# Both halves of an output projection as seven products instead of eight, in a fused attention and mixture-of-experts kernel

## The reference: what is computed

```
y_na  = neighbourhood_attention(q, k, v, rpb)          # (512 tokens, 512)
y_gla = gla_mixer(...)                                 # (512 tokens, 512)
x = x + concatenate([y_na, y_gla], axis=-1) @ w_out    # w_out: (1024, 1024)
h = rmsnorm(x, norm_ffn_g)
x = x + hierarchical_moe(h, ...)   # top group of 4, top 2 of its 8 experts; 32 experts, SwiGLU, width 512
return rmsnorm(x, final_norm_g)
```

## Time and profile before

| | us |
|---|---|
| median of 3 runs | 741.88 (740.94 to 743.22) |
| the profiled execution | 741.59 |
| its span, first to last instruction | 739.7 |
| PE busy / DVE busy / ACT busy / POOL busy in the span | 725.4 / 251.6 / 146.7 / 77.3 |
| moved by DMA in the span | 240.79 MB |

### The profile page before, as it was taken

The page is one execution under the profiler, slowest core; times in us unless marked ns, Lnnn a source line. Parts: engine busy times, 40 slices in busy tenths (PEclk is TensorE's granted clock), DMA queues, the critical chain, the costliest instruction groups (busy, mean ns, idle before and its releaser), DMA issues.

```text
span 739.7 us, 11649 instructions
## 1 busy us (share of the span) xinstructions
PE 725.4 (98%) x5077; PEld 403.3 (55%) x5077; DVE 251.6 (34%) x516; ACT 146.7 (20%) x315; POOL 77.3 (10%) x79
## 2 busy tenths in 40 slices
PE   9999999999999999999999999999999999999995
PEld 5488888888555564455454454444544544444431
DVE  2884463754873475112012012111111111111205
ACT  2652230134553541000000000000000000000014
POOL 0000049100000310000101001001000010010003
PEclk9999999999999999999999999999999999999999
DMA  9832322214902989999999999999999999999985
GB/s 322 265 113 101 141 103 86 86 67 178 390 2 85 424 293 388 414 429 426 414 419 427 436 431 433 433 428 430 439 414 424 434 424 426 426 427 426 422 362 232
DMA packets 31733, 240.79 MB, mean 326 GB/s; under 512 B 5590, under 2 KB 6998, under 8 KB 21184
## 3 DMA queue, kind: packets, MB, share of 16 engines
q1 hardware_dynamic: 29056, 235.94, 77.7%
q0 software_dynamic: 2480, 4.06, 1.5%
q10 hardware_dynamic: 144, 0.00, 0.0%
HBM read 231.74 MB, written 12.32 MB: 330 GB/s over the span
## 4 chain that ended last, share of the span: by engine, by line
PE 90%; DMA 7%; DVE 1%; ACT 1%; issue 0%; DVEq 0%
PE bank L1164 27%; PE bank L694 17%; PE bank L1184 14%; PE bank L1105 9%; DMA arena<-in_w_all 7%; PE bank L959 4%; PE bank L738 4%; PE bank L1008 4%; PE bank L1118 2%; PE bank L1173 1%; PE bank L997 1%; PE bank L911 1%; PE bank L978 1%; PE bank L1038 1%; PE bank L1219 1%; PE bank L888 1%
## 5 line engine op out<-in xcount | busy, mean ns | idle before, releaser
L1164 PE MATMUL bank<-arena 128*64 128x512 f32 x1024 | 226.7, 593 | 2.4 <-DMA arena<-in_w_all 2.3
L1164 PEld LDWEIGHTS bank<-arena 128*64 128x64 f32 x1024 | 73.4, 137 | 147.2 <-issue 147.0
L694 PE MATMUL bank<-arena 128*128 128x256 f32 x560 | 123.2, 380 | 0.0
L1184 PE MATMUL bank<-arena 128*64 128x512 f32 x512 | 116.9, 598 | 0.2
L694 PEld LDWEIGHTS bank<-arena 128*128 128x128 f32 x560 | 105.7, 190 | 15.5 <-issue 1.5
L1990 DVE SCALAR_TENSOR_TENSOR arena<-bank,arena 128x256 f32<-128x256 f32 x32 | 15.5, 484 | 215.4 <-ACT arena L1488 215.4
L1105 PEld LDWEIGHTS bank<-arena 128*128 128x128 bf16 x1344 | 75.3, 98 | 22.2 <-issue 21.9
L1534 DVE TENSOR_TENSOR arena<-arena 128x512 f32<-128x512 f32 (+8 forms) x105 | 81.2, 809 | 12.6 <-ACT arena L1305 6.1
L1488 ACT ACTIVATE arena<-bank,arena 128x256 f32<-128x256 f32 x32 | 15.2, 474 | 338.1 <-PE bank L1164 332.3
L1105 PE MATMUL bank<-arena 128*128 128x128 bf16 (+1 forms) x1344 | 81.6, 217 | 0.0
L2164 POOL DMA_INDIRECT y_tok<-arena x31 | 30.3, 978 | 402.4 <-DVE arena L1997 374.3
(11 more groups left out here) (179 smaller groups left out, 477.9 us busy)
## 6 DMA issues: line engine op xcount, KB each, us to landing
arena<-in_w_all SPq DMA_DIRECT2D x47, 2048.0 KB, 30.0
arena<-in_w_all SPq DMA_DIRECT2D x7, 6144.0 KB, 26.8
arena<-in_w_all SPq DMA_DIRECT2D x8, 4096.0 KB, 28.2
arena<-in_w_all SPq DMA_DIRECT2D x19, 1024.0 KB, 10.3
arena<-in_w_in SPq DMA_DIRECT2D x5, 2048.0 KB, 8.8
arena<-in_w_all SPq DMA_DIRECT2D x9, 512.0 KB, 7.8
arena<-in_x SPq DMA_DIRECT2D x8, 512.0 KB, 6.4
arena<-in_w_out SPq DMA_DIRECT2D x4, 1024.0 KB, 15.6
```

What stands on the lines that cost most here:

```text
L694: mm = pe.matmul(pbank[product_bank(g, p)][:, tile * 256:(tile + 1) * 256], lhs, rhs, start=(p in (1, 2, 5) and tile == 0 and k == 0), sto ...
L1164: mm = pe.matmul(both, xT[:, k, rows], gate_and_up(e, k)[:, :, cols], start=(k == 0), stop=(k == KC - 1))
L1184: mm = pe.matmul(pbank[down_bank(e)][64 * half:64 * half + 64, :], hidT[:, kc % 2, kc // 2], down_unit(e)[:, kc, half * 512:(half + 1) * 512],
```

## The change

Both halves become seven products of half-size blocks each, as in the input projection.

**GLA half.** For each half h of the 1024 columns, seven products (`SHARE_ORDER`), each of 256 tokens by 256 columns: 2 token tiles x 2 row chunks, 4 matmuls of 256 columns, in bank 4 or 5. 14 shares in 14 of the turns 3 to 18 (`SHARE_TURNS`; none in 8 and 13). DVE makes six sums of weight blocks ahead of the loop, four sums of token blocks in turn 2, one weight difference after each half's product 2, and 14 adds to `x1` (`add_share`), one for each product. To free banks 4 and 5 the scores of a pair of units now share banks 2 and 3, side by side; so the scores of both units wait until both units before have been read.

**Neighbourhood half.** For each pair m of token tiles, seven products (`NEAR_ORDER`), each of 128 tokens by 512 columns: 2 matmuls of 512 columns, 14 products. DVE makes three weight sums (`near_weight_sums`), four token sums per pair (`near_token_sums`, 256 elements in a row each), `last_near_sum`, and 14 adds (`add_near`). A half tile of `x1` is complete with the add named in `LAST_ADD`; in odd tiles the second half is complete first (`half_of`). The order of ScalarE's work stays, but for the last tile, where `hi(3,1)` comes ahead of the eviction. On DVE the order is written anew. On TensorE the new order is in the diff. `router` of the last tile starts with the half that DVE evicts.

**Loads.** Expert 1 waits for `pv_done` alone. Half of expert 2 (`load_half(2,0)`) lies over sums that the new form needs, and waits for product (1,6); other slices are cut and ordered anew.

```
-GLA_BANK = [0] * 6 + [2, 3]
+SHARE_ORDER = [(h, p) for h in range(2) for p in (1, 2, 6, 5, 7, 3, 4)]
+SHARE_TURNS = [3, 4, 5, 6, 7, 9, 10, 11, 12, 14, 15, 16, 17, 18]
+NEAR_ADDS = [(0, 1), (0, 2), (0, 5), (0, 6), (0, 3), (1, 2), (0, 7), (1, 1), (0, 4),
+             (1, 5), (1, 6), (1, 3), (1, 7), (1, 4)]
+LAST_ADD = {(0, 0): (0, 2), (0, 1): (0, 3), (1, 0): (0, 7), (1, 1): (0, 4),
+            (2, 0): (1, 1), (2, 1): (1, 3), (3, 0): (1, 7), (3, 1): (1, 4)}
+def near_bank(m, p):
+    return 2 if p == 2 else 1 if p in (5, 3) else 3 * m
+def half_of(t, n):
+    return n ^ t % 2
...
             sp.wait_ge(pv_done, 4 * PAIRS)
-            sp.wait_ge(og_done, 2 * TT)
             load_half(1, 0)
             load_half(1, 1)
             load_d(1)
-            load_half(2, 0)
-
             over_gla = slice(half_row // 2, half_row)
+            sp.wait_ge(og_done, len(SHARE_ORDER))
             sp.dma_start(flat_half(3, 1)[:, over_gla], half_d(3, 1)[:, over_gla]).then_inc(w2nd_in[3], 16)
+            sp.wait_ge(wo_done, near_product(0, 7))
             sp.dma_start(down_unit(2)[:, 2], down_d(2)[:, 2 * D:3 * D]).then_inc(wd_in[2], 16)
...
             load_over_residual(0)
+            sp.wait_ge(wo_done, max(near_product(0, 4), near_product(1, 1)))
             load_over_yT(0, 2)
+            load_over_w_on(0, 1)
             load_over_residual(1)
+            sp.wait_ge(wo_done, max(near_product(1, 5), near_product(1, 6)))
+            load_half(2, 0)
+            sp.wait_ge(wo_done, near_product(1, 3))
+            load_over_w_on(3, 4)
+            load_over_residual(2)
+            sp.wait_ge(wo_done, len(NEAR_ORDER))
+            load_over_w_on(1, 3)
             load_over_yT(2, 3)
-            load_over_w_on(0)
-            load_over_residual(2)
-            load_over_w_on(1)
             load_over_yT(3, 4)
             load_over_residual(3)
...
             def na_scores(i):
                 pair, b = divmod(i, BLOCKS)
-                if i >= 2:
-                    pe.wait_ge(s_added, 2 * (i - 1))
+                if i >= 2 and i % 2 == 0:
+                    pe.wait_ge(s_added, 2 * i)
...
             def gla_share(n):
+                h, p = SHARE_ORDER[n]
+                if n >= 2:
+                    pe.wait_ge(og_added, n - 1)
+                if p in (3, 4, 5, 6, 7):
+                    pe.wait_ge(sums_done, max(sums("Y", {5: 1, 6: 2, 7: 3}.get(p, 4)), sums(f"share{h}", 4 if p == 4 else 2)))
+                a, w = share_tokens(p), share_weights(h, p)
+                for tile in range(2):
+                    for k in range(2):
+                        mm = pe.matmul(pbank[share_bank(h, p)][:, tile * 256:(tile + 1) * 256], a[:, k, tile * P:(tile + 1) * P],
+                                       w[:, k], start=(p in (1, 2, 5) and tile == 0 and k == 0), stop=(tile == 1 and k == 1),
+                                       skip_group_check=p in (6, 7, 4, 3))
+                mm.then_inc(og_done, 1)
...
+            def out_proj(m, p, ks=range(2)):
+                before = {6: 1, 7: 6, 4: 7, 3: 5}.get(p)
+                if before and ks[0] == 0:
+                    pe.wait_ge(og_added, near_added(m, before))
+                if m == 1 and p in (2, 5) and ks[0] == 0:
+                    pe.wait_ge(og_added, near_added(0, 2 if p == 2 else 3))
+                if p in (3, 4, 5, 6, 7) and ks[0] == 0:
+                    pe.wait_ge(sums_done, max(sums(("y", m), {5: 1, 6: 2, 7: 3}.get(p, 4)), sums("N", 4 if p == 4 else 2)))
...
+            pe.wait_ge(wout_in, 32)
+            pe.wait_ge(yn_evicted, PAIRS // 2)
+            out_proj(0, 1)
             pe.wait_ge(yn_evicted, PAIRS)
+            pe.wait_ge(s_added, 2 * NU)
+            out_proj(0, 2)
+            out_proj(0, 5)
+            out_proj(0, 6)
+            out_proj(0, 3)
+            out_proj(1, 2)
+            out_proj(0, 7)
             x1_T(0)
+            out_proj(1, 1)
+            out_proj(0, 4)
             pe.wait_ge(router_ready, 3)
             router(0)
+            out_proj(1, 5)
             x1_T(1)
+            out_proj(1, 6)
             router(1)
+            out_proj(1, 3)
+            out_proj(1, 7)
             x1_T(2)
+            out_proj(1, 4, range(0, 1))
             router(2)
...
             ranks(0, 2)
+            out_proj(1, 4, range(1, 2))
             last_x1_T(0)
             last_x1_T(1)
...
             def hi(t, n):
+                half = half_of(t, n)
+                act.wait_ge(og_added, x1_half(t, n))
...
             (DVE)
+            near_token_sums(0)
+            add_near(0, 1)
+            add_near(0, 2)
+            add_near(0, 5)
             rest(0, 0)
+            add_near(0, 6)
+            add_near(0, 3)
+            near_token_sums(1)
             rest(0, 1)
+            add_near(1, 2)
+            last_near_sum()
+            add_near(0, 7)
             mean_square(0)
+            x1_T_evict(0)
             rest(1, 0)
+            add_near(1, 1)
             inverse_root(0)
+            add_near(0, 4)
             rest(1, 1)
+            add_near(1, 5)
+            x1_T_evict(1)
             mean_square(1)
+            add_near(1, 6)
             rest(2, 0)
             inverse_root(1)
+            add_near(1, 3)
+            route_groups(0, 2)
             rest(2, 1)
+            add_near(1, 7)
+            x1_T_evict(2)
             mean_square(2)
             route_experts(0, 2)
             rest(3, 0)
             inverse_root(2)
             route_groups(2, 3)
             route_experts(2, 3)
+            add_near(1, 4)
             first_slots(0, 2)
             x1_T_evict(3)
             rest(3, 1)
```

More of the change, by code:

```diff
@@ L140, in second_half_landed @@
 def second_half_landed(e):
-    return landed(e, lambda n: 32 if n == 2 or n in IN_HALVES else 16, 64)
+    return landed(e, lambda n: 48 if n == 2 else 32 if n in IN_HALVES else 16, 64)
 def down_landed(e):
@@ L910, in na_scores @@
                     k0 = KEY_START[b] * ROWS
-                    mm = pe.matmul(pbank[2 + 2 * (i % 2) + par][:, 0:NKEY], na_q[rows, pair, b * P:(b + 1) * P],
+                    mm = pe.matmul(pbank[2 + par][:, i % 2 * NKEY:(i % 2 + 1) * NKEY], na_q[rows, pair, b * P:(b + 1) * P],
                                    na_k[rows, pair, k0:k0 + NKEY], start=True, stop=True)
@@ new lines, in y_sums @@
+            def y_sums():
+                low, high = slice(0, 2), slice(2, 4)
+                dve.wait_ge(yg_evicted, GLA_HEADS)
+                tt(y_sum[1], yT_gla[:, low, late], yT_gla[:, high, late], ALU.add).then_inc(sums_done, 1)
+                tt(y_sum[3], yT_gla[:, low, early], yT_gla[:, low, late], ALU.subtract).then_inc(sums_done, 1)
+                dve.wait_ge(sums_done, sums("Y", 1))
+                tt(y_sum[2], y_sum[1], yT_gla[:, low, early], ALU.subtract).then_inc(sums_done, 1)
+                dve.wait_ge(sums_done, sums("Y", 2))
+                tt(y_sum[4], yT_gla[:, high, early], y_sum[2], ALU.subtract).then_inc(sums_done, 1)
@@ new lines, in add_share @@
+            def add_share(n):
+                h, p = SHARE_ORDER[n]
+                if n == 0:
+                    for t in range(TT):
+                        dve.wait_ge(x_in_sb[t], 32)
+                dve.wait_ge(og_done, n + 1)
+                if n:
+                    dve.wait_ge(og_added, n)
+                tt(share_target(h, p), share_target(h, p), pbank[share_bank(h, p)][:].rearrange("p (t c) -> p t c", t=2),
+                   ALU.add).then_inc(og_added, 1)
+                if p == 2:
+                    dve.wait_ge(sums_done, sums(f"share{h}", 2))
+                    tt(share_quarter(h, 1, 0), share_quarter(h, 1, 0), share_sum[h][2], ALU.subtract).then_inc(sums_done, 1)
@@ L1744, in _ @@
                     scale_probs(1)
+                    y_sums()
                     join(NEAR_V, 5)
@@ L1909, in _ @@
             route_experts(2, 3)
-            residual(3, 1)
+            add_near(1, 4)
             first_slots(0, 2)
@@ L2154, in _ @@
             for t in range(TT):
-                for half in range(2):
-                    pool.wait_ge(mid_done, 2 * t + half + 1)
+                for n in range(2):
+                    half = half_of(t, n)
+                    pool.wait_ge(mid_done, 2 * t + n + 1)
                     nc.gpsimd.tensor_tensor(h2_part[t][2][:, halves[half]], rest2[t % 2][:, halves[half]],
```

208 lines of the change are left out of this document (122 added, 86 removed).

## The result

The kernel after took 749.85 us (median of 6, 748.77 to 751.67), the kernel before beside it 742.55 (6 runs, 740.94 to 744.12): ratio 1.0101, 95% interval 1.0081 to 1.0122. I had forecast 743.0, from 738.5 to 746. The profiled execution took 750.87 (span 749.1). One execution of the kernel before, beside a later experiment, took 4285.84 us; it stands in no ratio.

The account below looks back on a forecast made before the run. The weight queue's deciding issue after the router stage was taken as the bound, TensorE next. Issue +1.05 and expert 0 +1.5 (-3.4 + 0.35 + 4.0 + 0.55) gave +1.2 us: 743.0, range 738.5 to 746.

Parts of the forecast that it names:

- the paragraph on the clock: TensorE ahead of two routers: gaps of 2.75 us leave the clock at 2.4 GHz, so nothing was added.
- rival C: Router stage: the clock falls to half behind two gaps, about +10 us, 753; chance 3%.
- GLA half, work and banks: Score loop: 14 shares of 1.85 us instead of 16 of 1.83, -3.4 us; shared score banks +0.35 us.
- The charge of 0.35 us: Score loop, turn 14: scores come 0.3 us too soon for DVE; +0.35 us charged, bounds 0 and 3 us.
- the waits, places, releasers and sizes: Neighbourhood half: TensorE waits at four places, 2.15, 2.75, 1.35 and 1.95 us, together 8.2 us.
- the stage: First neighbourhood product to expert 0: 231.9 to 279.9 us; to the last transposes 40.5 us, +4.0, then router(3) +0.55.
- the sum: End of the run: deciding issue +1.05, expert 0 on TensorE +1.5; +1.2 us taken.
- the deciding issue: Weight queue after the router stage: the issue from which it never runs dry, moving from 275.58 to 276.6 us, +1.05.
- Rival A: Both halves: the saved work arrives at the end, -6.8 us, 735.1, if all four waits are hidden; chance 15%.
- Rivals B and D: B: DVE sets the score loop's pace, 745.0, 16%. D: weight slices land after 278 us, 2 us late, 745, 5%.

Follow-up runs that it names:

- e2: Kernel after, with ScalarE's three evictions of the transposes moved forward in its queue: 741.96 us, ratio 0.9997 to the kernel before.
- e3: Kernel before, with router(0) also waiting for rest(2,0), a gap of 2.2 us on TensorE: 745.63 us, ratio 1.0061.
- e6: Kernel before, with router(0) also waiting for hi(2,0), a shorter gap of 1.48 us on TensorE: 744.57 us, ratio 1.0041.
- e1: Kernel after, with useless 320-column matmuls in TensorE's four gaps and all waits kept: 744.08 us, ratio 1.0034 to the kernel before.
- e4: Kernel before, with the GLA half of the change alone, the neighbourhood half as before: 738.41 us, ratio 0.9953.
- e5: Kernel after, with ScalarE's three evictions moved ahead and four useless matmuls ahead of the last transposes: 739.42 us, ratio 0.9978 to the kernel before.
- e8: Kernel after, with evictions moved ahead, four useless matmuls, and DVE's route_groups(0,2) ahead of product (1,3)'s add: 738.37 us, ratio 0.9958 to the kernel before.
- e7: Kernel before, with router(0) also waiting for rest(2,0) and three useless matmuls ahead of that wait: 743.35 us, ratio 1.0028.

## Why the prediction was wrong

**The step that failed** is the paragraph on the clock: "Through 4.8 us of standing still it was at 2.4 GHz, so gaps of 2.75 us leave it there, and I add nothing", and with it the 3% of rival C. The row was read rightly: at the end of the run the clock fell 4.8 us after PE's last matmul. The inference was wrong. It took the time from PE's stop to the fall for the length of standing still that a fall needs. In the kernel after, the fall came 2.8, 4.8 and 3.2 us after PE's last record ahead of a gap had ended, in e2 3.0, in e3 and e6 2.7, and all six times PE had taken up work again by then, 0.2 to 2.3 us before: the fall comes behind the gap and does not ask whether it is over. A row in which nothing follows cannot show that. Nor is 4.8 us a fixed length. The same instructions end every run; in e1 the clock fell 3.0 us after the last of them, in the kernel after 5.3, in e6 2.6 (PE's last record ends at 734.62, the fall is at 737.2):
```profile
734.00:737.00 3.00, 0.63 (x2) 0.00 (x0) 1.44 (x3) 2.95 (x6) 2.78 (x2) 1.00 0.54 210
737.00:738.00 1.00, 0.00 (x0) 0.00 (x0) 0.56 (x2) 0.99 (x2) 0.00 (x0) 0.60 0.97 389
```
Rival C had the mechanism, not the price: it put 10 us on two gaps. The clock fell three times, and e1, where it stays, takes 7.3 us off the stage and 5.0 off the end, by the two ratios, whose intervals are some 1.5 and 1.1 us to either side. Its rule, which the prediction named from the Trainium skill ("TensorE: Matmul & The Clock Gate", "Why this matters for your kernels"), that idle gaps between bursts of matmuls bring the clock back to half, is borne out by these runs. The row there speaks of longer gaps than any of these; where it and the runs differ the runs decide, and in e6 1.48 us was enough.

**Right:** GLA half, work and banks. A share takes 1.83 us (the last one runs from 230.17 to 232.00; forecast 1.85), and S is 232.0. The charge of 0.35 us was for scores that wait for DVE at turn 14. They do not wait: the loop loses 0.18 us, and that one turn earlier, where transposes wait for ScalarE's copy:
```profile
215.42 0.63 PE L1065 MATMUL bank<-arena 128*128 128x128 f32 x4 [0.18 <-ACT arena L1512]
```
e4 shows that this part reaches the end whole, within its interval.

**Right:** the waits, places, releasers and sizes. Ahead of router(0) 2.01 (2.15), of router(1) 2.52 (2.75), around x1_T(2) 0.17 + 0.97 = 1.14 (1.35). The last, 1.02 instead of 1.95, is short since PE, at half rate, came late to it; at full clock, in e1, three fillers and 0.46 us stand there, 2.24 us from start to start. In e1 the four come to 8.7 us with the fillers in them, forecast 8.2.

**Off by 0.7 us:** the stage. 48.71 in e1 against 48.0 (279.9 - 231.9); 0.5 of it is in the four gaps. And e1's ratio, 1.0034, is 2.5 us, where the sum gave 1.2; its interval (1.4 to 3.6) leaves out 1.2 by little.

**What the end follows:** the prediction let the deciding issue set it, PE's start of expert 0 second. Over the eleven profiled executions the time less E0 is 462.8 to 464.7 us, the time less the deciding issue 465.6 to 469.3. The odd one is e2: its issue came at 273.48, 2.1 us earlier than before's, expert 0 at 278.59, 0.2 later, and its time equals before's. There E0 tells the time better, though this is one kernel, and PE waits longer for weights in it (3.2 us, before 2.3). In the kernel after both were late by 7.5 to 9.6 us.

**Rival A** asked too little: it wanted the four waits hidden. e2 hides the two of ScalarE's queue, and the saved 3.44 us still do not arrive; DVE's chain of adds and routing (e5, e8) takes the place. I had treated DVE's part as one late add of 1.95 us, not as the stage's next bound. **Rivals B and D** did not happen: the score loop runs to plan, and PE waits for weights 2.0 us.

**Left open:** how much of a gap, and next to what, makes the clock fall. Single gaps of 0.54 us in e7 and up to 0.69 in e2 did not, 1.48 in e6 did, and probably not in each of its runs; between them nothing was tried. The delay to the fall (2.6 to 5.3 us, the ends of the runs with it) is open too. The stretches at half rate differ in length (3.4 to 10.2 us) without going by the length of the gap: 6.8 us behind 2.01, 3.4 behind 2.52.

## What to carry to other kernels

A wait on TensorE can be paid twice, by its length and by the clock behind it: here gaps of 6.7 us in all were followed by half rate that cost 5 to 7 us more. So when a change shortens TensorE's work between two dependencies, look first for what else can stand there; useless matmuls in the gaps kept the clock up in the profiled execution (e1), and an earlier place for the evictions in ScalarE's queue took the two largest gaps away as well (from e1 to e5, both at full clock, the stage is 4.6 us shorter). And saved work counts only up to the next engine's chain: before trading products for adds, add up the other engine's rows in that stage from its first dependent instruction to the last.

## What the runs showed of the hardware

Behind the six gaps that a fall followed, the granted clock fell 2.7 to 4.8 us after TensorE stopped, each time when it was at work again, and stayed at half for 3.4, 6.8 or 10.2 us while TensorE was busy nearly all along. In the kernel after it was still 1.00 5 us after the last matmul, which ends at 740.96, and fell at 746.3; in e6 it fell 2.6 us after (above):
```profile
741.00:746.00 5.00, 0.00 (x0) 0.00 (x0) 2.40 (x5) 3.62 (x6) 1.91 (x1) 1.00 0.55 216
746.00:749.00 3.00, 0.00 (x0) 0.00 (x0) 0.00 (x0) 0.00 (x0) 0.00 (x0) 0.54 0.73 280
```
At half rate a four-instruction product of 512 columns took 3.55 us instead of 1.72, a router 3.41 instead of 1.71. The 72 bfloat16 matmuls of 64 columns took 3.2 instead of 2.1, the last 0.8 us of it at full rate again; at half rate the trace has 46 of them in 2.3 us, at full rate 73 in 2.0, so these are slowed 1.8 times, not twice. In every run of the kernel after the mean clock was 0.984 to 0.987, before's 0.995 to 0.998, so the mean over the whole run, three digits long, already told the two apart. It does not tell a single gap so surely: e6's seven runs go from 0.992 to 0.997.
